# A mixture-of-experts encoder block: the router on raw rows, another order on three engines, and block 0's list ahead of the tables

## The chip, the cores and the metric

The kernel runs on one core of a Trainium2 chip. Its time is device time in microseconds (us) from the start to the end of the program on that core; a run is one execution, and the number given is the median of several. The engines are named as in the profile: PE (TensorE, matrix products), PEld (its weight loads), DVE (VectorE), ACT (ScalarE), POOL (GpSimd) and SP (SyncE, which here only issues DMAs).

## The reference

One layer works on 528 tokens (16 meta tokens and 512 others) of width 1024, in float32:

```
n    = rmsnorm(h, attn_norm); proj = n @ w_in           # 1024 x 3072
o    = stick_breaking_attention (8 heads) | differential_attention (4 heads)
h    = h + o @ w_out
xf   = rmsnorm(h, ffn_norm)
logits = xf @ w_router + b_router                       # 32 experts
top 4 of 32 per token, gates = softmax of the four logits
for each expert: act = clamped_swiglu(xf[tok] @ w1[e] + b1[e]); y = act @ w2[e] + b2[e]
h    = h + sum of gate * y over a token's four experts
out  = rmsnorm(h, final_norm), meta tokens dropped
```

w1 is 1024 x 2048 and w2 1024 x 1024 per expert, so the 32 experts' weights are 403 MB, and each is read once.

## The kernel before

The program is written by hand for each engine, in order; semaphores join them. It has four stages.

1. Projection and attention, from 0 to about 320 us. The change does not touch them beyond places of constants.
2. The tokens' stage, in four tiles of 128 tokens (t = 0 to 3). PE adds the differential heads' part of the output projection in eight units u of 512 columns (`out_tile`, L1447, two units a tile). DVE adds the residual (`token_rows`, L992), ACT squares and sums (L728) and takes the root by logarithm and exponential (`rsqrt`, L584 and L585), DVE refines the root in four small steps (L801 to L804) and writes the normed row, times the gain, to a stage buffer (L997). SP stores the raw rows to `accd` (L443) and the normed rows to `xfd` (L446), the table in memory that blocks gather from. PE turns the normed rows (`turn_tokens`, L1470), ACT copies them out of PSUM (L739), PE forms the 32 logits (`logits`, L1481), DVE adds the bias, finds the four largest and makes a 0/1 mask (L1008 to L1016), and from ACT's exponentials (L745) the gates in three bfloat16 parts with the token's number (L1018 to L1028).
3. The tables. PE counts tokens per expert and ranks each token within its expert (L1496 to L1500). DVE turns counts into numbers of 32-slot blocks; experts are put in an order ("places") through two small products (L1503, L1505); then tables by block are made (L1066 to L1082), after which `tab_ready` lets every engine read the number of blocks into a register.
4. The experts, 81 blocks of 32 slots. For block n: DVE compares ranks with slot numbers (`slot_list(n)`, L1097, L1101), PE's small product gathers token numbers and gates (`slot_product(n)`, L1527), DVE makes indices (`slot_rows(n)`, L1109 to L1122), POOL gathers rows from `xfd` (L535), PE turns them (`turn_x`, L1521), ACT copies (L751), PE multiplies by w1 (`up`, L1546) with a bias product at the end (L1553), DVE and ACT form the activation, PE turns it (L1583) and multiplies by w2 (`down`, L1573), DVE applies gates (L1142) and POOL adds rows to `accd` (L543). Lists run four blocks ahead; the list of a block and its product share one buffer, so `slot_list(n + 1)` waits for `slot_product(n)`.

Weights go through two buffers, one for even and one for odd places. SP issues an expert's four loads of w1 (L469) and two of w2 (L474) in the loop, each after PE has read that part for the buffer's last user. The first expert's weights and half of the second's w1 are loaded before the tables; the rest of the second's (L418 and L461) waits for `tab_ready` and block 0's gather.

## Time and profile before

| | |
|---|---|
| three runs | 1431.04 us median (1430.64 to 1434.6) |
| profiled execution | 1431.11 us, of which span 1429.3 |
| PE busy | 1302.9 us, 91% of the span |
| DVE, ACT, POOL busy | 670.1, 291.4, 284.3 us |
| mean granted clock of PE | 0.963 of full |
| DMA | 459.65 MB, mean 322 GB/s |

The span runs from the first to the last instruction. Busy shares are means over stages: a wait matters only where it ends last. A group's "idle before" is the time its engine stood still ahead of its instructions, with what ended most of it; "issue" there means that no wait of the profile explains it. SPq is the queue of DMA issues.

### The profile page before, as it was taken

To read this page: it belongs to the slowest core of one execution; us is meant where nothing else is said; L and a number is where in the kernel's file an instruction comes from. 1 tells how busy PE (TensorE), PEld (TensorE's weight loads), DVE (VectorE), ACT (ScalarE), POOL (GpSimd) and SP (SyncE) were. 2 spreads that over 40 slices of the span, in tenths; PEclk is the share of its full clock that TensorE was granted. 3 is DMA by queue.
4 is the path that set the end of the run, shared out by engine and by line. 5 is a ranking of instruction groups with operands and counts; after the bars stand their busy time and mean duration, and the time that the engine had idled before them with its cause. 6 is when DMAs were issued, how large, how long until landed. Compare 5 with 4: busy or idle time off the path is not lost.

```text
span 1429.3 us, 36690 instructions
## 1 busy us (share of the span) xinstructions
PE 1302.9 (91%) x13312; PEld 623.7 (44%) x13313; DVE 670.1 (47%) x2257; ACT 291.4 (20%) x578; POOL 284.3 (20%) x455
## 2 busy tenths in 40 slices
PE   4999999989288997899999999997999899999992
PEld 2655666555233442344444444442444344444441
DVE  3015333664644553355555555553455355555555
ACT  3102223432011111111111111111111111111113
POOL 5400000000012222122222222222222122222221
PEclk9999999999589999999999999998999999999996
DMA  9520001617478999999999998999999999999995
GB/s 317 157 50 1 1 1 63 236 27 312 158 313 337 415 417 418 419 416 416 417 418 417 417 417 319 378 413 417 419 416 417 422 416 417 417 418 417 415 416 185
DMA packets 59808, 459.65 MB, mean 322 GB/s; under 512 B 8420, under 2 KB 8804, under 8 KB 27012
## 3 DMA queue, kind: packets, MB, share of 16 engines
q1 hardware_dynamic: 51220, 436.63, 73.8%
q0 software_dynamic: 8176, 22.36, 6.0%
q8 instruction: 19, 0.31, 0.1%
q10 hardware_dynamic: 384, 0.26, 0.1%
q14 instruction: 9, 0.07, 0.0%
HBM read 440.72 MB, written 18.51 MB: 321 GB/s over the span
## 4 chain that ended last, share of the span: by engine, by line
PE 83%; DMA 9%; DVE 4%; issue 2%; ACT 1%; POOL 0%; SPq 0%; DVEq 0%; POOLq 0%; ACTq 0%
PE PS L1546 37%; PE PS L1573 19%; DMA sb_arena<-in_w 7%; PE PS L1227 4%; PE PS L1233 4%; PE PS L1583 2%; PE PS L1230 2%; PE PS L1231 2%; PE PS L1422 2%; PE PS L1447 1%; PE PS L1521 1%; PE PS L1589 1%; PE PS L1553 1%; PE PS L1329 1%; PE PS L1395 1%
## 5 line engine op out<-in xcount | busy, mean ns | idle before, releaser
L1546 PE MATMUL PS<-sb_arena,sb_work 128*32 128x512 f32 x5184 | 586.7, 603 | 35.3 <-DMA sb_arena<-in_w 28.6
L1546 PEld LDWEIGHTS PS<-sb_arena,sb_work 128*32 128x32 f32 x5184 | 174.2, 111 | 398.1 <-issue 347.4
L1573 PE MATMUL PS<-sb_arena,sb_work 128*32 128x256 f32 x5184 | 296.5, 380 | 4.6
L1129 DVE TENSOR_SCALAR sb_work<-PS 128x256 f32<-128x256 f32 x81 | 34.4, 425 | 395.8 <-PE PS L1553 395.8
L1573 PEld LDWEIGHTS PS<-sb_arena,sb_work 128*32 128x32 f32 x5184 | 166.3, 110 | 111.1 <-issue 19.4
L769 ACT ACTIVATE sb_work<-PS 128x256 f32<-128x256 f32 x81 | 31.1, 384 | 810.9 <-PE PS L1583 810.9
L1142 DVE TENSOR_SCALAR sb_work<-PS,sb_gates 32x256 f32<-32x256 f32 x324 | 155.2, 479 | 15.0 <-PE PS L1573 0.8
L534 POOL TENSOR_TENSOR sb_sm<-sb_sm 128x1 f32<-128x1 f32 x85 | 16.9, 199 | 676.9 <-DVE sb_gidx L1120 676.9
L1097 DVE TENSOR_SCALAR sb_slots<-sb_ca,sb_b,sb_rk 128x128 bf16<-128x128 f32 x344 | 96.5, 370 | 59.0 <-issue 58.2
L543 POOL DMA_INDIRECT accd<-sb_work,sb_sidc x81 | 111.1, 1371 | 12.5 <-issue 1.1
L767 ACT ACT_TABLE_LOAD x81 | 103.9, 1283 | 1.4
L535 POOL DMA_INDIRECT sb_work<-xfd,sb_gidx x85 | 86.2, 1014 | 14.0 <-issue 3.8
L1227 PE MATMUL PS<-sb_arena 128*128 128x512 f32 x128 | 60.1, 613 | 0.6 <-DVE sb_work L833 0.6
L1233 PE MATMUL PS<-sb_arena 128*128 128x512 f32 x128 | 58.6, 598 | 1.0 <-DVE sb_arena L851 1.0
L542 POOL TENSOR_TENSOR sb_sm<-sb_sm 128x1 f32<-128x1 f32 x81 | 15.7, 194 | 213.1 <-DVE sb_sidc L1144 213.1
L879 DVE TENSOR_TENSOR_SCAN sb_arena<-sb_arena 128x1344 f32<-128x1344 f32 x8 | 23.7, 2958 | 53.5 <-ACT sb_arena L639 53.5
L1583 PEld LDWEIGHTS PS<-sb_ca,sb_work 128*128 128x128 f32 x162 | 25.5, 206 | 53.2 <-issue 53.2
L1132 DVE TENSOR_TENSOR sb_work<-sb_work,PS 128x256 f32<-128x256 f32 x81 | 34.1, 421 | 29.7 <-ACT PS L756 29.6
L1583 PE MATMUL PS<-sb_ca,sb_work 128*128 128x128 f32 x162 | 40.9, 334 | 1.6 <-issue 1.5
L1230 PE MATMUL PS<-sb_arena 128*128 128x264 f32 x128 | 39.3, 389 | 0.0
L1231 PE MATMUL PS<-sb_arena 128*128 128x264 f32 x128 | 38.9, 386 | 0.0
L1521 PE MATMUL PS<-sb_ca,sb_work 128*128 128x128 f32 x166 | 33.9, 286 | 5.0 <-DMA sb_work<-xfd,sb_gidx 5.0
(246 smaller groups left out, 1165.8 us busy)
## 6 DMA issues: line engine op xcount, KB each, us to landing
sb_arena<-in_w SPq DMA_DIRECT2D x192, 2048.0 KB
sb_arena<-in_w_in SPq DMA_DIRECT2D x6, 2048.0 KB, 21.4
sb_arena<-in_x SPq DMA_DIRECT2D x8, 512.0 KB, 9.6
sb_arena<-in_w_out SPq DMA_DIRECT2D x2, 2048.0 KB, 13.1
accd<-sb_arena SPq DMA_DIRECT2D x4, 512.0 KB, 7.6
xfd<-sb_arena SPq DMA_DIRECT2D x4, 512.0 KB, 5.8
sb_arena<-accd SPq DMA_DIRECT2D x4, 512.0 KB, 5.0
out<-sb_arena SPq DMA_DIRECT2D x4, 512.0 KB, 3.5
```

What stands on the lines that cost most here:

```text
L535: pool.indirect_dma_start(out=xg[b], out_offset=None, in_=xfd, in_offset=bass.IndirectOffsetOnAxis(ap=gidx[:, b:b + 1], axis=0)).then_inc( ...
L543: pool.indirect_dma_start(out=acc, out_offset=bass.IndirectOffsetOnAxis(ap=sidc[0:SLOTS, b:b + 1], axis=0), in_=yb[b], in_offset=None, com ...
L767: act.preload_act_table(ACT.Sigmoid)
L1097: nc.vector.tensor_scalar(slots[:, t, :].rearrange("p (q s) -> p q s", s=SLOTS), ca[:, C_SLOT:C_SLOT + SLOTS].unsqueeze(1).to_broadcast([P ...
L1142: nc.vector.tensor_scalar(yb[b][:, c * QD:(c + 1) * QD], PS[rows, 4, 0:QD], gates[rows, bass.ds(n, 1)], None, ALU.mult).then_inc(y_ready, 1)
L1227: last = mm(PS[:, b, :], w[:, k, f * P:(f + 1) * P], nT[:, k, META:NKEY], **io)
L1230: mm(PS[:, b, 0:n], w[:, k, f * P:(f + 1) * P], nT[:, k, 0:n], **io)
L1231: last = mm(PS[:, b + 1, 0:n], w[:, k, f * P:(f + 1) * P], nT[:, k, n:NKEY], **io)
L1233: last = mm(PS[:, b, :], nT[:, k, META + f * P:META + (f + 1) * P], w[:, k, :], **io)
L1546: last = mm(PS[group(c), b, :].rearrange("p (a n) -> p a n", a=2), xT[:, k % 2, group(k // 2)], w[:, k, :, c, :], start=k == 0, stop=False)
L1573: last = mm(PS[group(n), 4, 0:QD], actT[:, k % 2, group(k // 2)], w[:, k, n * QD:(n + 1) * QD], start=False, stop=k == KT - 1)
L1583: last = nc.tensor.transpose(PS[:, 6, j * P:(j + 1) * P], pairs(gat[b], j), ident)
```

## The change

- *Raw rows.* The router's product works on `res`, the rows before the norm. The norm's gain vector is multiplied into the router's weights once (POOL, `wr` times `fcol`, a new small load), and the root's factor is applied to the logits as DVE reads them (first line of `choose`). Turning tokens no longer waits for the norm. The normed rows for `xfd` are now made by ACT (scale by the root) and POOL (times the gain).
- *Order.* Units of projection, turns and logits alternate on PE; DVE and ACT have their steps in a written-out order; `choose` and `weigh` are apart, with all 32 exponentials kept and masked. The last tile's turned rows are copied by DVE in two halves. The token numbers in `g6` are written by POOL at the start.
- *Tables.* Block 0 belongs to expert 0 from rank 0, so its list needs no table: DVE lists it (`slot_places(0, 0.0)`), PE multiplies, DVE makes its indices, and POOL gathers it while the tables are made. Slot numbers start from 1 so that a rank needs no subtraction. `slot_list(1)` comes before the last tables.
- *Start of the experts.* PE, ACT and POOL read the number of blocks later; on PE after block 0's `up`, and `slot_product(2)` is now behind it too. SP's wait for the gather is one for block 0's turn.
- Small buffers lie elsewhere in the work area.

```diff
-    a[:, C_SLOT:C_SLOT + SLOTS] = np.arange(SLOTS)
+    a[:, C_SLOT:C_SLOT + SLOTS] = 1 + np.arange(SLOTS)
...
-            sp.wait_ge(xg_in[0], 16)
+            sp.wait_ge(xT_done, 1)
...
+            pool.wait_ge(rout_in, 48)
+            nc.gpsimd.tensor_tensor(wr, wr, fcol.unsqueeze(2).to_broadcast([P, KT, NE]), ALU.mult)\
+                .then_inc(wr_ready, 1)
+            pool.wait_ge(gain_in, 32)
+            for t in range(TT):
+                pool.wait_ge(scaled, t + 1)
+                nc.gpsimd.tensor_tensor(stage[t % 2], stage[t % 2], gain, ALU.mult).then_inc(xf_ready, 1)
 
...
-            def token_norm(t):
+            def token_root(t):
                 act.wait_ge(h_ready, 2 * (t + 1))
                 if t >= 2:
-                    act.wait_ge(xfT_done, t - 1)
...
+            def token_scale(t):
+                act.wait_ge(root_ready, t + 1)
+                act.activation(stage[t % 2], res[:, t, :], ACT.Copy, scale=rinv[:, t:t + 1]).then_inc(scaled, 1)
+
+            def token_copy(t):
...
+            token_root(0)
+            token_scale(0)
+            token_root(1)
+            token_copy(0)
+            token_scale(1)
+            choice_exp(0)
+            token_root(2)
+            token_copy(1)
+            token_scale(2)
+            token_copy(2)
+            choice_exp(1)
+            choice_exp(2)
+            token_root(3)
+            token_scale(3)
+            choice_exp(3)
...
+            def choose(t):
                 dve.wait_ge(lg_done, t + 1)
                 if t == 0:
+                    dve.wait_ge(rout_in, 48)
+                row = lg[:, t, :]
+                nc.vector.scalar_tensor_tensor(row, PS[:, 6 + t % 2, 0:NE], rinv[:, t:t + 1], br,
+                                               ALU.mult, ALU.add).then_inc(lg_read, 1)
+                dve.wait_ge(lg_read, t + 1)
+                step(nc.vector.max(v8, row))
+                nc.vector.tensor_scalar(ntop[:, t:t + 1], v8[:, 0:1], -1.0, None, ALU.mult).then_inc(e4_in, 1)
+                step(nc.vector.max_index(i8u, v8, row))
                 step(nc.vector.tensor_copy(i8f, i8u[:, 0:TOPK]))
                 ie = ct[:, T_IE:T_IE + NE].unsqueeze(1).to_broadcast([P, TOPK, NE])
                 step(nc.vector.tensor_tensor(oh, i8f.unsqueeze(2).to_broadcast([P, TOPK, NE]), ie, ALU.is_equal))
+                step(nc.vector.tensor_reduce(gr[:, t, :], oh.rearrange("p k e -> p e k"), AX.X, ALU.add))
+                nc.vector.tensor_copy(msk[:, t, :], gr[:, t, :]).then_inc(msk_ready, 1)
+
+            def weigh(t):
+
+                row, part = e32[:, t, :], [g6[:, t, :, i] for i in range(3)]
                 dve.wait_ge(e4_ready, t + 1)
...
+            token_rows(0)
+            token_rows(1)
+            token_root(0)
+            token_rows(2)
+            token_rows(3)
+            token_root(1)
+            token_rows(4)
+            choose(0)
+            token_rows(5)
+            weigh(0)
+            token_root(2)
+            token_rows(6)
+            choose(1)
+            weigh(1)
+            choose(2)
+            token_rows(7)
+            for half in range(2):
+                dve.wait_ge(xfT_done, 2 * TT - 1 + half)
+                dve.wait_ge(lg_done, TT - 2)
+                nc.vector.tensor_copy(stT[1][:, 4 * half:4 * half + 4, :],
+                                      PS[:, 4 + half, :].rearrange("p (k n) -> p k n", k=4)).then_inc(xfT_ready, 1)
+            token_root(3)
+            choose(3)
+            weigh(2)
...
             step(nc.vector.tensor_copy(nb2[:, 0:1], nblk))
-            step(nc.vector.tensor_copy(nb2[:, 1:2], onesb[0:NE, 0:1]))
-            step(nc.vector.tensor_scalar(erep, onesb[0:NE, :], ca[0:NE, C_EXP:C_EXP + 1], None, ALU.mult))
-            step(nc.vector.tensor_copy(ee[:, 0:1], ca[0:NE, C_EXP:C_EXP + 1]))
+            weigh(3)
             dve.wait_ge(codes_done, 1)
...
+            dve.wait_ge(rank_done, 2)
+            step(nc.vector.scalar_tensor_tensor(rk[:, :, :], PS[:, 6, 64:64 + P].rearrange("p (t e) -> p t e", t=TT),
+                                                1.0, msk, ALU.add, ALU.mult))
+            dve.wait_ge(g6_ready, TT)
+            slot_places(0, 0.0)
+            step(nc.vector.tensor_scalar(at, ie0, place, None, ALU.is_equal))
+            dve.wait_ge(places_done, 1)
+            nc.vector.tensor_scalar(later, PS[0:NE, 7, 0:NE], place, None, ALU.is_ge).then_inc(nb_ready, 1)
+            step(nc.vector.memset(c6[:, :], 0.0))
+            slot_rows(0, 0, 0)
...
+            step(nc.vector.tensor_copy(egf[:, :], PS[:, 5, 256:256 + NG]))
+            step(nc.vector.tensor_copy(etab[:, :], egf[0:1, :]))
+            step(nc.vector.tensor_tensor(b64[:, :], ct[:, T_I32:T_I32 + NG], PS[:, 5, 128:128 + NG], ALU.subtract))
+            step(nc.vector.tensor_copy(prow, PS[0:1, 5, 0:NG]))
+            slot_list(1)
+            step(nc.vector.scalar_tensor_tensor(ptab[:, :], prow[:, 2:NG], float(AHEAD), prow[:, 0:NG - 2],
+                                                ALU.mult, ALU.add))
+            step(nc.vector.tensor_copy(order[:, :], PS[0:1, 4, NE:2 * NE]))
+            step(nc.vector.tensor_copy(btabi[:, :], PS[0:1, 4, 0:NE]))
+            nc.vector.memset(nx, 0.0).then_inc(tab_ready, 1)
+
...
+                for half in range(2):
+                    pe.wait_ge(h_ready, 2 * t + 1 + half)
+                    if t >= 1 and half == 0:
+                        pe.wait_ge(xfT_ready, t)
+                    for k in range(4 * half, 4 * half + 4):
+                        last = nc.tensor.transpose(PS[:, 4 + half, (k % 4) * P:(k % 4 + 1) * P],
+                                                   res[:, t, k * P:(k + 1) * P], ident)
+                    last.then_inc(xfT_done, 1)
...
+            for u in range(4):
+                out_part(u, 0, HF)
+            turn_tokens(0)
+            out_part(4, 0, HF)
+            logits(0)
+            out_part(5, 0, HF)
+            turn_tokens(1)
+            out_part(6, 0, HF)
+            turn_tokens(2)
+            logits(1)
+            out_part(7, 0, 2)
+            logits(2)
+            out_part(7, 2, HF)
+            turn_tokens(3)
+            logits(3)
...
+                if t == 0:
+                    pe.wait_ge(msk_ready, TT - 1)
                 for t2 in range(t):
                     mm(dst, onesb, msk[:, t2, :], start=t2 == 0, stop=False)
+                if t == TT - 1:
+                    pe.wait_ge(msk_ready, TT)
+                    for t2 in range(TT):
+                        last = mm(PS[0:NE, 7, 0:1], msk[:, t2, :], onesb[:, 0:1], start=t2 == 0, stop=t2 == TT - 1)
+                    last.then_inc(rank_done, 1)
...
+            slot_product(0)
             pe.wait_ge(nb_ready, 1)
             mm(PS[0:NE, 7, 0:2], later, nb2, start=True, stop=True).then_inc(bs_done, 1)
...
+            turn_x(0, 0, 0)
+            slot_product(1)
+            pe.wait_ge(xT_ready, 1)
+            up(0, 0, 0, 0)
             pe.wait_ge(tab_ready, 1)
             nb = pe.value_load(btabi[0:1, NE - 1:NE], min_val=1, max_val=MAXBLK)
-            slot_product(0)
-            turn_x(0, 0, 0)
-            slot_product(1)
-            pe.wait_ge(list_ready, 2)
             slot_product(2)
-            pe.wait_ge(xT_ready, 1)
-            up(0, 0, 0, 0)
             turn_x(1, 1, 0)
             slot_product(3)
```

How instructions stand on the engines, "[waits ...]" naming semaphores. First PE, end of the tokens' stage. L1447 is a unit of projection (four columns of k), L1481 logits, L1470 a turn. Before:

```order
L1447 MATMUL PS<-sb_arena 128x512 [waits h_ready]
L1447 MATMUL PS<-sb_arena 128x512 x3
L1481 MATMUL PS<-sb_arena 128x32 [waits e4_in,xfT_ready]
L1481 MATMUL PS<-sb_arena 128x32 x7
L1470 MATMUL PS<-sb_ca,sb_arena 128x128 [waits xfT_ready,xf_ready]
L1470 MATMUL PS<-sb_ca,sb_arena 128x128 x7
L1481 MATMUL PS<-sb_arena 128x32 [waits e4_in,xfT_ready]
L1481 MATMUL PS<-sb_arena 128x32 x7
L1470 MATMUL PS<-sb_ca,sb_arena 128x128 [waits xfT_ready,xf_ready]
L1470 MATMUL PS<-sb_ca,sb_arena 128x128 x7
L1481 MATMUL PS<-sb_arena 128x32 [waits e4_in,xfT_ready]
L1481 MATMUL PS<-sb_arena 128x32 x7
```

With the change (L1509 projection, L1548 logits, L1534 a turn, in halves):

```order
L1509 MATMUL PS<-sb_arena 128x512 [waits h_ready]
L1509 MATMUL PS<-sb_arena 128x512
L1548 MATMUL PS<-sb_arena 128x32 [waits xfT_ready,lg_read]
L1548 MATMUL PS<-sb_arena 128x32 x7
L1509 MATMUL PS<-sb_arena 128x512 x2
L1534 MATMUL PS<-sb_ca,sb_arena 128x128 [waits xfT_ready,h_ready]
L1534 MATMUL PS<-sb_ca,sb_arena 128x128 x3
L1534 MATMUL PS<-sb_ca,sb_arena 128x128 [waits h_ready]
L1534 MATMUL PS<-sb_ca,sb_arena 128x128 x3
L1548 MATMUL PS<-sb_arena 128x32 [waits xfT_ready,lg_read]
L1548 MATMUL PS<-sb_arena 128x32 x3
L1548 MATMUL PS<-sb_arena 128x32 [waits xfT_ready]
```

The last turn and last logits had nothing between them and waited on the norm (`xf_ready`); now half units of projection stand between the logits of tiles 1 and 2 and the last turn, which waits for the raw rows (`h_ready`), and the last logits come in two halves.

Second DVE, from the experts' places on. Before (L1060 the key of places, L1063 to L1071 ends of experts, from L1073 tables):

```order
L1060 TENSOR_SCALAR sb_work<-sb_ca,sb_work 32x32 [waits dve_step]
L1061 TENSOR_SCALAR sb_work<-sb_work 32x32
L1063 TENSOR_SCALAR sb_work<-PS,sb_work 32x32 [waits places_done,dve_step]
L1066 COPY sb_work<-PS 32x1 [waits bs_done]
L1067 CAST sb_work<-sb_work 32x1 [waits dve_step]
L1068 TENSOR_TENSOR sb_work<-sb_work 32x1 [waits dve_step]
L1069 TENSOR_SCALAR sb_work<-sb_work 32x102 [waits dve_step]
L1070 TENSOR_SCALAR sb_work<-sb_work 32x102 [waits dve_step]
L1071 TENSOR_TENSOR sb_work<-sb_work 32x102 [waits dve_step]
L1073 COPY sb_egf<-PS 128x102 [waits tab_done]
L1074 COPY sb_work<-PS 1x102 [waits dve_step]
L1075 SCALAR_TENSOR_TENSOR sb_ptab<-sb_work 1x100 [waits dve_step]
```

With the change (L1115 the key, L1157 ranks, L1121 and L1125 the list, L1161 and L1163 ends, L1140 on the indices):

```order
L1115 TENSOR_SCALAR sb_work<-sb_ca,sb_work 32x32 [waits dve_step]
L1157 SCALAR_TENSOR_TENSOR sb_rk<-PS,sb_work 128x128 [waits rank_done]
L1121 TENSOR_SCALAR sb_slots<-sb_ca,sb_rk 128x128 [waits g6_ready,dve_step]
L1121 TENSOR_SCALAR sb_slots<-sb_ca,sb_rk 128x128 x3
L1125 COPY sb_g6c<-sb_g 128x24
L1161 TENSOR_SCALAR sb_work<-sb_work 32x32
L1163 TENSOR_SCALAR sb_work<-PS,sb_work 32x32 [waits places_done,dve_step]
L1164 MEMSET sb_c 128x9
L1140 COPY sb_c<-PS 128x6 [waits list_done,dve_step]
L1142 TENSOR_SCALAR sb_c<-sb_c 128x1 [waits list_step]
L1144 TENSOR_SCALAR sb_c<-sb_c,sb_ca 128x1
```

Block 0's list and indices have moved from behind all tables to a place ahead of them.

Third PE, around blocks 0 and 1. L1527 is a list's product, L1546 and L1553 block 0's first expert product, L1521 the turn of block 1's rows, L1532 a register load. Before:

```order
L1527 MATMUL PS<-sb_g6c,sb_slots 128x6 [waits slots_ready,list_ready]
L1527 MATMUL PS<-sb_g6c,sb_slots 128x6 x3
L1546 MATMUL PS<-sb_arena,sb_work 32x512 [waits w1_full00,xT_ready]
L1546 MATMUL PS<-sb_arena,sb_work 32x512 x7
...
L1553 MATMUL PS<-sb_ball,sb_selb 32x512 [waits sel_ready]
L1553 MATMUL PS<-sb_ball,sb_selb 32x512 x3
L1521 MATMUL PS<-sb_ca,sb_work 128x128 [waits xT_ready,xg_in1]
L1521 MATMUL PS<-sb_ca,sb_work 128x128
L1527 MATMUL PS<-sb_g6c,sb_slots 128x6 [waits slots_ready]
L1527 MATMUL PS<-sb_g6c,sb_slots 128x6 x3
L1532 TENSOR_LOAD sb_ptab
```

With the change (L1588, L1626 and L1633, L1607, L1612; L1679 is the load of the number of blocks):

```order
L1626 MATMUL PS<-sb_arena,sb_work 32x512 [waits w1_full00,xT_ready]
L1626 MATMUL PS<-sb_arena,sb_work 32x512 x7
...
L1633 MATMUL PS<-sb_ball,sb_selb 32x512 [waits sel_ready]
L1633 MATMUL PS<-sb_ball,sb_selb 32x512 x3
L1679 TENSOR_LOAD sb_btabi [waits tab_ready]
L1679 ISA x2
L1588 MATMUL PS<-sb_g6c,sb_slots 128x6 [waits slots_ready]
L1588 MATMUL PS<-sb_g6c,sb_slots 128x6 x3
L1607 MATMUL PS<-sb_ca,sb_work 128x128 [waits xT_ready,xg_in1]
L1607 MATMUL PS<-sb_ca,sb_work 128x128
L1588 MATMUL PS<-sb_g6c,sb_slots 128x6 [waits slots_ready]
L1588 MATMUL PS<-sb_g6c,sb_slots 128x6 x3
```

Behind block 0 there are now a register load and two list products instead of one, list 2's and list 3's, with block 1's turn between.

## Rows read from the trace of the kernel before

**Rows 1.** The page: clock and DMA by 36 us slices, costliest group.
```profile
PEclk9999999999589999999999999998999999999996
DMA  9520001617478999999999998999999999999995
...
L1546 PE MATMUL PS<-sb_arena,sb_work 128*32 128x512 f32 x5184 | 586.7, 603 | 35.3 <-DMA sb_arena<-in_w 28.6
```

**Rows 2.** Busy times by 30 us windows; columns as in the first row.
```profile
core 0: us, PE busy (x) PEld busy (x) DVE busy (x) ACT busy (x) POOL busy (x), PEclk, DMA share, GB/s
440.00:470.00 30.00, 29.89 (x348) 11.84 (x338) 12.27 (x44) 4.49 (x8) 6.01 (x10) 0.97 0.81 326
...
860.00:890.00 30.00, 29.83 (x368) 13.09 (x364) 14.01 (x51) 6.21 (x12) 7.47 (x12) 1.00 0.77 296
```

**Rows 3.** The same view in windows of 4 us.
```profile
372.00:376.00 4.00, 0.58 (x14) 0.46 (x14) 3.42 (x17) 0.00 (x0) 0.00 (x0) 0.50 1.01 426
380.00:384.00 4.00, 0.57 (x5) 0.30 (x5) 2.87 (x14) 0.00 (x0) 0.00 (x0) 0.50 0.00 2
...
444.00:448.00 4.00, 3.94 (x48) 1.65 (x44) 0.93 (x3) 0.86 (x3) 0.00 (x0) 1.00 0.24 102
```

**Rows 4.** Timeline of the DMA-issuing queue (start us, us, queue, line).
```profile
392.41 0.82 SPq L418 DMA_DIRECT2D sb_arena<-in_w  x2
...
453.83 1.49 SPq L469 DMA_DIRECT2D sb_arena<-in_w  x2
```

**Rows 5.** Timeline of PE, blocks 3 and 4; in brackets the idle time before.
```profile
437.25 9.20 PE L1546 MATMUL PS<-sb_arena,sb_work 128*32 128x512 f32 x64 [5.48 <-issue]
...
451.17 7.05 PE L1546 MATMUL PS<-sb_arena,sb_work 128*32 128x512 f32 x64
```

**Rows 6.** Chain of waits, the tokens' stage (start us, us, what).
```profile
320.16 14.00 PE PS L1447 x32
334.16 0.87 PE PS L1470 x8
335.04 6.87 PE PS L1447 x16
341.90 1.72 PE PS L1481 x16
```

**Rows 7.** Timeline of DVE: the choice of the last 128 tokens.
```profile
369.94 0.19 DVE L1008 TENSOR_TENSOR sb_arena<-PS,sb_arena 128x32 f32<-128x32 f32 x1 [2.46 <-PE PS L1481]
...
371.69 0.18 DVE L1016 CAST sb_work<-sb_arena 128x32 bf16<-128x32 f32 x1
```

**Rows 8.** Timeline of ACT: turned copy, squares, last step of the root.
```profile
345.09 1.00 ACT L739 ACTIVATE sb_arena<-PS 128x1024 f32<-128x1024 f32 x1
349.51 1.06 ACT L728 ACTIVATE sb_arena<-sb_arena 128x1024 f32<-128x1024 f32 x1 [3.42 <-DVE sb_arena L992]
...
351.01 0.20 ACT L585 ACTIVATE sb_sm<-sb_sm 128x1 f32<-128x1 f32 x1
```

**Rows 9.** DMA view, 331 to 333 us; the last number is us to landing.
```profile
xfd<-sb_arena SPq DMA_DIRECT2D x1, 512.0 KB, 14.2
```

**Rows 10.** Timeline of DVE: a register load, and block 0's indices.
```profile
384.95 0.07 DVE L1147 MEMSET sb_c<- 128x9 f32 x1 [0.88 <-issue]
...
388.38 0.21 DVE L1120 TENSOR_SCALAR sb_gidx<-sb_c 128x1 int32<-128x1 f32 x1
```

**Rows 11.** Chain of waits from block 0's gather to block 1.
```profile
389.49 2.84 DMA sb_work<-xfd,sb_gidx
...
396.65 8.98 PE PS L1546 x64
...
407.56 2.76 PE PS L1546 x21
```

**Rows 12.** DMA view, 399 to 402 us, the gather queue.
```profile
q0 software_dynamic: 48, 0.13, 10.9%
```

**Rows 13.** Groups by line, POOL: its widest two-input operation.
```profile
L511 POOL TENSOR_TENSOR sb_arena<-sb_arena,sb_ball 32x1024 f32<-32x1024 f32 x3 | 7.2, 2404 | 0.3
```

255 lines of the change are left out of this document (108 added, 147 removed).

## Prediction, written before the changed kernel ran

> **What bounds the kernel now.** I read the page first, then windows, then the chain. The page's slices show a long stretch, from about 460 us to the end, in which the DMA engines are full and PE is nearly so; its costliest group, the first expert product, lost 35.3 us idle, 28.6 of them to weights [rows 1]. So two things bound the experts' stage, PE and the weight stream, and the question is where each last waited for the other. The 30 us windows answer it: from 860 to 890 us PE is full while the DMA share is 0.77 (the stream waits for PE to free a buffer), and from 440 to 470 it is 0.81 [rows 2]. The fine windows find the earliest such gap, DMA share 0.24 at 444 to 448 us [rows 3], and the queue's timeline ends it: the loads for the fourth expert are issued at 453.83, once PE has read the buffer in block 4 [rows 4], whose product begins at 451.17 [rows 5]. From there on both engines run on each other. Before there, nothing is full: the stream stood idle, so it is PE's blocks 0 to 4 that set when everything later happens. **A microsecond won before block 4 is won at the end**, and the sum only has to say how much earlier block 4 starts.
>
> Block 0 starts at 396.65 [rows 11] and waits for a chain with no slack: PE projects and turns tokens (320.16 to 343.6, [rows 6]), then DVE and PE hand one another short work. In 372 to 376 us DVE is busy 3.42 us with 17 instructions, in 380 to 384 us 2.87 us with 14 [rows 3]: 31 in 8 us, 0.26 us per link, and PE idles at clock 0.5, the lower of its two levels, 1.2 GHz. This latency chain is what the change rewrites.
>
> **Term 1, the tokens' stage.** Before, the last choice starts at 369.94 and its mask is cast at 371.69 to 371.87, 1.93 us after it began [rows 7]. After, I walk PE's new list. Four units of projection take 14.00, a full turn 0.87, one unit half of 6.87, so 3.44, logits of 128 tokens 1.72 [rows 6]. 320.16 + 14.00 + 0.87 + 3.44 (unit 4) + 1.72 (logits 0) + 3.44 (unit 5) + 0.87 (turn 1) + 3.44 (unit 6) = 347.9. All that these wait for is earlier: the raw rows are turned, so no turn waits for the norm, and the copy of turn 0 is ready at about 337.8. Then one wait is left. ACT's third square writes over the stage of tile 0 and must wait for that tile's store, which landed 14.2 us after its issue at 332 [rows 9], behind 8 MB of weights; the store is now issued some 2 us later (POOL multiplies by the gain) but queues behind the same weights, so I keep 346.2. Square and root take 1.7 (349.51 to 351.21), the copy behind them 1.0 [rows 8]: 349.0, a stall of 1.1 on PE. Turn 2, logits 1, half of unit 7, logits 2, other half: 0.87 + 1.72 + 1.72 + 1.72 + 1.72 from 349.1 gives 356.9. DVE's add (0.7), squares and root on ACT (1.7) and DVE's refining (four links, 0.9) come to 360.3; on the other branch half a turn and two copies of 0.7 each feed the last half of the logits, done at about the same time. Choice 1.93: the last mask is there at 362.5. Gain 371.87 - 362.5 = 9.4. PE is denser until 357, so its clock can hardly fall earlier than it did.
>
> **Term 2, from the last mask to block 0's indices.** Before: 371.87 to 388.59 = 16.7 [rows 7, 10], with all tables, two register loads and the list in it. After, DVE's row holds 39 instructions: 7 weigh(2), 3 counts, 2 code and key, 2 bf16 copies, 7 weigh(3), 3 rank, place and key, 1 rank table, 5 slots, 3 small ones, 6 of the list. At 0.24 to 0.26 us each plus about 0.3 for PE's product this is 9.7. The two weigh calls sit ahead of waits that PE has already met, so they cost about 3 us on the path, yet less than the tables did. Gain 7.0. Indices at 372.2, gather issued 0.9 later (388.59 to 389.49), 373.1. The four tables' stores are no limit: POOL's two-input operation of 1024 columns takes 2.4 us [rows 13], so the last store goes out near 365 and lands by 371. If its price grew with partitions (32 there, 128 here) it would be 9.6 us, four in a row from 332 end at 370.4, the store lands near 375.5, and the end comes 2.4 us later.
>
> **Term 3, the gather.** Before it flew alone, 2.84 us [rows 11]. After, it meets the 4 MB of w2 loads that are issued right behind the last store and run until about 377. The next gather did meet such a stream: issued at 395.21, its packets ran only between 399 and 402 [rows 12], 6.5 us. Bounds 2.84 and 6.5; I take 5.4, since the stream ends meanwhile. Loss 2.6: it lands at 378.5. The Trainium skill, "DMA: Bandwidth & Descriptors", queues and rings, says that each DMA engine takes turns between queues packet by packet. By that rule a gather of few packets should be held up by one or two weight packets only, about 1 us, and land near 377, which would make the end 1.5 us earlier; the gather of [rows 12] disagrees.
>
> **Term 4, landing to block 0.** Before 392.33 to 396.65 = 4.3, because the product of list 2 was ahead of block 0. After only the turn (0.7), ACT's copy and their hops, 1.4; list 1, ahead of it on PE, is ready at about 377.5. Gain 2.9. Block 0 starts at 379.9, 16.7 us earlier (9.4 + 7.0 - 2.6 + 2.9). It ends 9.2 later, at 389.2, since its clock starts low as before.
>
> **Term 5, a new serial wait between block 0 and block 1.** PE's row now has, behind block 0: register load, product of list 2, turn 1, product of list 3, register load and branch. List 3 is written by DVE only after it has read the product of list 2, and before the change block 0's 9 us hid that. Now nothing does: register load 0.9 (DVE's took 0.88, [rows 10]), product 0.3, DVE's rows 1.3, list 3 1.8 (1.12 of slots, 0.48 of register load and the copy), product 0.3, load and branch 1.2: 5.8. Before, block 0's end at 405.9 to block 1 at 407.56 [rows 11] was 1.7. Loss 4.1. Block 1 at 395.0, 12.6 earlier. Queued behind PE here is everything; DVE's first activation only waits with it.
>
> **Term 6, the clock.** PE is idle for more than 5 us there. In block 3 it was idle 5.48 and the product took 9.20; the next took 7.05 at full clock [rows 5]. Block 1 took 7.07 before, so I charge 2.15; bounds 0 and 2.15. Block 1 ends 10.4 us earlier.
>
> Block 2 follows without a gap, and block 3's idle 5.48 stays. The stream's second expert is issued after the tables and block 0's turn, about 379.5 in place of 392.41 [rows 4], 20 us of loads, so it is done near 400 and block 3, near 427, does not wait. POOL's token columns, the extra router load and the longer constants lie beside waits: POOL's own first work after the attention stage is block 0's gather, and the loads go out with the first experts'. I take 0, bounds 0 and 0.5.
>
> **Sum.** The profiled execution took 1431.11 (span 1429.3 plus 1.8 around it; the runs' median is 1431.04, the same). 1431.1 - 9.4 - 7.0 + 2.6 - 2.9 + 4.1 + 2.15 = **1420.6 us**.
>
> **Rivals.** *A, more is won:* the gather flies as if alone (2.6 back), PE's clock stays (2.15 back), DVE's links go at 0.24 (0.8 back): 1415.0. For it: loads may drain first. Against: [rows 12], [rows 5].
>
> *B, the stream decides:* if the weights bound everything from their second start, only 392.41 - 379.5 = 12.9 counts, 1418.2. Against it: DMA share 0.24 and 0.00 in [rows 3].
>
> *C, one more stall for instructions:* PE's idle 5.48 ahead of block 3 is put down to nothing it waits for, and block 3 is the first to run the other parity's copy of the code, behind a taken branch, with the DMA engines full [rows 5]. After the change PE reaches the code of block 0 and 1 with the stream running, while before it sat idle with quiet DMA engines first. One such stall costs 5.48 + 2.15 = 7.6: 1428.2. The Trainium skill ("Runtime: NRT & Kernel Launch", instruction fetch mechanics) says that prefetch is sequential and that a taken branch outside of the fetched pages waits for a DMA. By that rule block 3's stall stays and the straight code of block 0 is safe; the trace agrees as far as block 3 goes.
>
> *D, slower:* the same stall in two places, ahead of block 0's product and at block 1's branch, 15.2: 1435.8. It decides once stalls sum to more than 10.5 us. Nothing in the trace shows two.
>
> **Chances.** Forecast 0.65 (its own range 1416 to 1425), A 0.15, B 0.05, C 0.11, D 0.04. A measurement of this kernel tells apart about 0.3%, 4.3 us: faster (forecast, A, B) 0.85, same (C) 0.11, slower (D) 0.04. Range 1413 to 1428.5: A with room below for both weigh calls being cheaper, C at the top.
>
> **What would show it.** The last mask near 362.5; block 0's indices near 372 and its product near 380; PE idle about 5 us between blocks 0 and 1 with DVE's list 3 as releaser, and block 1's product at 9.2; the same gap in the DMA windows ahead of block 4's release, now near 443; all later waits of PE for weights as long as before. The forecast is wrong if the block 0 start moves by under 12 us, or if the later idle time of the expert products grows.

## The result, and the profile after

| | before | after |
|---|---|---|
| median | 1431.39 us (1429.61 to 1434.6, 8 runs) | 1420.83 us (1418.35 to 1426.62, 8 runs) |
| profiled execution | 1431.11 us, span 1429.3 | 1421.65 us, span 1419.7 |
| mean granted clock of PE | 0.963 | 0.972 |

The ratio is 0.9928, 95% interval 0.9912 to 0.9944: faster by 0.7%. The forecast was 1420.6. In a second set, beside some of its variants, the same kernel had 1421.46 us (1419.45 to 1423.19, 5 runs), ratio 0.9939 (0.9926 to 0.9951).

The page of the kernel after, clock and DMA by slices and the costliest group, against [rows 1]:

```profile
PEclk9999999999699998999999999999999999999997
DMA  8520000607678999999999998999999999999995
...
L1626 PE MATMUL PS<-sb_arena,sb_work 128*32 128x512 f32 x5184 | 587.2, 604 | 36.9 <-DMA sb_arena<-in_w 29.9
```

The first expert product lost 36.9 us idle where it had lost 35.3, its waits for weights 29.9 where they had been 28.6. The prediction had named growing idle time there as a sign against it. It cost nothing: from block 4's start to the end of the span it is 978.3 us after and 978.1 before, so what was won ahead of block 4 was still there at the end. Windows of the kernel after (PE, PEld, DVE, ACT and POOL busy, PEclk, DMA share, GB/s), against [rows 3]:

```profile
436.00:440.00 4.00, 3.94 (x64) 2.28 (x60) 2.59 (x11) 2.25 (x4) 0.00 (x0) 1.00 0.02 8
```

Ahead of the release of the next weight buffer the DMA share was 0.02: the stream waited for PE, as at 444 to 448 us in [rows 3]. The queue of DMA issues, against [rows 4]:

```profile
382.06 0.81 SPq L423 DMA_DIRECT2D sb_arena<-in_w  x2
...
443.77 5.22 SPq L475 DMA_DIRECT2D sb_arena<-in_w  x4
```

The second expert's loads are issued 10.35 us earlier, the release in block 4 10.06 us earlier. PE's timeline after, against [rows 5, 11] (L1576 counts tokens, L1607 turns a block's rows, L1588 is a list's product, L1626 a block's first expert product):

```profile
365.55 0.27 PE L1576 MATMUL PS<-sb_work 128*32 128x1 bf16 x4 [3.55 <-DVE sb_work L1052]
...
381.27 0.70 PE L1607 MATMUL PS<-sb_ca,sb_work 128*128 128x128 f32 x2 [5.23 <-DMA sb_work<-xfd,sb_gidx]
...
382.44 9.36 PE L1626 MATMUL PS<-sb_arena,sb_work 128*32 128x512 f32 x64 [0.39 <-ACT sb_work L784]
...
391.95 0.25 PE L1588 MATMUL PS<-sb_g6c,sb_slots 128*128 128x6 bf16 x4
...
395.43 0.25 PE L1588 MATMUL PS<-sb_g6c,sb_slots 128*128 128x6 bf16 x4 [2.88 <-DVE sb_g6c L1125]
396.87 8.77 PE L1626 MATMUL PS<-sb_arena,sb_work 128*32 128x512 f32 x64 [1.19 <-ACT sb_work L784]
...
410.36 7.05 PE L1626 MATMUL PS<-sb_arena,sb_work 128*32 128x512 f32 x64
...
427.83 8.86 PE L1626 MATMUL PS<-sb_arena,sb_work 128*32 128x512 f32 x64 [5.51 <-issue]
...
441.41 7.05 PE L1626 MATMUL PS<-sb_arena,sb_work 128*32 128x512 f32 x64
```

Block 0 is 14.2 us earlier than in [rows 11] (396.65), block 1 10.7 (407.56), and blocks 3 and 4 9.4 and 9.8 against [rows 5]. Three more views show what stood behind it. The chain of waits after, the store of the first tile and block 0's gather, against [rows 9, 11]:

```profile
335.11 12.08 DMA xfd<-sb_arena
...
374.99 6.23 DMA sb_work<-xfd,sb_gidx
```

ACT after, its third square, waiting for that store, against [rows 8]:

```profile
347.27 1.06 ACT L744 ACTIVATE sb_arena<-sb_arena 128x1024 f32<-128x1024 f32 x1 [5.27 <-DMA xfd<-sb_arena]
```

DVE after, the last choice (L1042 to L1052) and block 0's indices, and POOL's multiply beside it, against [rows 7, 10, 13]:

```profile
358.32 0.18 DVE L1052 CAST sb_work<-sb_arena 128x32 bf16<-128x32 f32 x1
...
361.89 0.25 DVE L1042 SCALAR_TENSOR_TENSOR sb_arena<-PS,sb_sm,sb_arena 128x32 f32<-128x32 f32 x1 [0.17 <-PE PS L1548]
...
363.30 0.38 DVE L1051 TENSOR_REDUCE sb_arena<-sb_arena 128x32 f32<-128x128 f32 x1
363.70 1.79 DVE L1052 CAST sb_work<-sb_arena 128x32 bf16<-128x32 f32 x1
...
373.88 0.21 DVE L1151 TENSOR_SCALAR sb_gidx<-sb_c 128x1 int32<-128x1 f32 x1
```
```profile
362.98 2.48 POOL L544 TENSOR_TENSOR sb_arena<-sb_arena 128x1024 f32<-128x1024 f32 x1 [9.45 <-ACT sb_arena L751]
```

The mask's cast takes 1.79 us in the last tile and 0.18 in the third. It ends at 365.49, POOL's multiply at 365.46.

### The profile page after: what moved, and what is told of

The parts are those of the page before. It is cut to its first block, busy times and chain, and to the rows that moved or that the text cites. A ratio compares the mean times of both kernels' runs of the same rounds, so it can differ in the third digit from the quotient of the medians.

```text
span 1419.7 us, 36680 instructions
## 1 busy us (share of the span) xinstructions
PE 1299.2 (92%) x13312; PEld 620.4 (44%) x13313; DVE 660.7 (47%) x2241; ACT 294.6 (21%) x577; POOL 296.1 (21%) x464
## 4 chain that ended last, share of the span: by engine, by line
PE 82%; DMA 10%; DVE 4%; issue 2%; ACT 1%; POOL 0%; SPq 0%; DVEq 0%; POOLq 0%; ACTq 0%
PE PS L1626 37%; PE PS L1653 19%; DMA sb_arena<-in_w 7%; PE PS L1290 4%; PE PS L1296 4%; PE PS L1663 2%; PE PS L1293 2%; PE PS L1294 2%; PE PS L1485 2%; PE PS L1607 1%; PE PS L1669 1%; PE PS L1633 1%; PE PS L1392 1%; PE PS L1458 1%; DMA xfd<-sb_arena 1%
## 5 line engine op out<-in xcount | busy, mean ns | idle before, releaser
L1626 PE MATMUL PS<-sb_arena,sb_work 128*32 128x512 f32 x5184 | 587.2, 604 | 36.9 <-DMA sb_arena<-in_w 29.9
L1626 PEld LDWEIGHTS PS<-sb_arena,sb_work 128*32 128x32 f32 x5184 | 174.7, 111 | 399.8 <-issue 348.8
L1196 DVE TENSOR_SCALAR sb_work<-PS 128x256 f32<-128x256 f32 x81 | 34.3, 424 | 398.8 <-PE PS L1633 398.8
L551 POOL TENSOR_TENSOR sb_sm<-sb_sm 128x1 f32<-128x1 f32 x85 | 16.7, 197 | 552.5 <-DVE sb_gidx L1151 552.5
L1121 DVE TENSOR_SCALAR sb_slots<-sb_ca,sb_b,sb_rk 128x128 bf16<-128x128 f32 x340 | 96.1, 367 | 59.2 <-issue 59.2
L552 POOL DMA_INDIRECT sb_work<-xfd,sb_gidx x85 | 85.8, 1009 | 14.1 <-issue 3.8
L1607 PE MATMUL PS<-sb_ca,sb_work 128*128 128x128 f32 x166 | 33.9, 286 | 5.2 <-DMA sb_work<-xfd,sb_gidx 5.2
```

The costliest lines, as they stand in the source:

```text
L552: pool.indirect_dma_start(out=xg[b], out_offset=None, in_=xfd, in_offset=bass.IndirectOffsetOnAxis(ap=gidx[:, b:b + 1], axis=0)).then_inc( ...
L1121: nc.vector.tensor_scalar(slots[:, t, :].rearrange("p (q s) -> p q s", s=SLOTS), ca[:, C_SLOT:C_SLOT + SLOTS].unsqueeze(1).to_broadcast([P ...
L1626: last = mm(PS[group(c), b, :].rearrange("p (a n) -> p a n", a=2), xT[:, k % 2, group(k // 2)], w[:, k, :, c, :], start=k == 0, stop=False)
```

## Experiments

Each kernel is the changed one with the edit shown. "Set" means kernels that ran together and share their runs of the kernel before. Only one set holds the changed kernel too (the second one above, with the mask's product, w2 behind the gather and the squares apart), so across sets the ratios are to be compared.

One thing bears on all of them: PE's projection of the tokens' stage began anywhere from 318.22 to 322.10 us in the profiles of the changed kernel and its variants, a spread that the edits do not explain. Where it matters, the start is given.

### Raw rows undone, order kept

```diff
-            nc.gpsimd.tensor_tensor(wr, wr, fcol..., ALU.mult)
+            nc.gpsimd.tensor_copy(wr, wr)
...
-    scalar_tensor_tensor(row, PS[...], rinv[:, t:t + 1], br, ...)
+    scalar_tensor_tensor(row, PS[...], 1.0, br, ...)
...
             token_rows(7)
+            token_root(3)
             for half in range(2):
...
-            token_root(3)
             choose(3)
...
-                    pe.wait_ge(h_ready, 2 * t + 1 + half)
+                    pe.wait_ge(xf_ready, t + 1)
...
-                        res[:, t, k * P:(k + 1) * P], ident)
+                        stage[t % 2][:, k * P:(k + 1) * P], ident)
```

DVE's order is not quite kept: the last tile's root now stands ahead of the two copies of its turned rows, which wait for the norm here.

> The changed kernel with one part undone: PE turns the normed rows (it waits for POOL's last step of the norm), the router's weights are not multiplied by the gain, and the logits are not scaled. The order on every engine stays. The output is unchanged. Own theory (turning raw rows is what takes the norm off the path): PE stalls at turn 2 for about 3.5 us more and the last turn waits for root (2.0), scale (1.1) and POOL's 2.4 us, about 6 us more; the 1.6 us that DVE's last mask lost beside POOL may come back. Together about +8 us: last mask near 373, PE's block 0 product near 390, time about 1428.8. Rival (the new order alone gives the gain, the norm is hidden by it): 0 to +2 us, 1421 to 1423.

Measured: 1434.88 us (1431.41 to 1438.56, 12 runs), ratio to before 1.0027 (1.0016 to 1.0039). That is 14 us above the changed kernel, not 8. PE and clock in this kernel:

```profile
352.70 1.97 PE L1534 MATMUL PS<-sb_ca,sb_arena 128*128 128x128 f32 x8 [4.21 <-POOL sb_arena L544]
...
364.56 3.76 PE L1509 MATMUL PS<-sb_arena 128*128 128x512 f32 x4
...
375.33 1.97 PE L1534 MATMUL PS<-sb_ca,sb_arena 128*128 128x128 f32 x8 [7.00 <-POOL sb_arena L544]
...
397.13 8.72 PE L1626 MATMUL PS<-sb_arena,sb_work 128*32 128x512 f32 x64
```
```profile
352.00:356.00 4.00, 3.30 (x16) 3.30 (x17) 0.00 (x0) 1.02 (x1) 0.65 (x1) 0.59 0.32 131
356.00:360.00 4.00, 4.00 (x13) 2.89 (x13) 1.83 (x11) 0.32 (x1) 0.00 (x0) 0.50 0.00 0
```

Both stalls are there as expected (4.21 and 7.00 us). What I left out is that the first of them lets the clock fall to 0.50, so half a unit of projection takes 3.76 us in place of 1.96, and every step up to the last logits takes about twice as long. The last mask is there at 382.94, not near 373: 17.5 us later than in the changed kernel and 11.1 later than before the change. Block 0's list ahead of the tables and the shorter way from the landing to block 0 win 10.6 of these 11.1 back, so block 0 is 0.5 later than before the change (14.7 later than in the changed kernel), and the new wait behind it makes block 1 3.4 later. So the new order loses in the tokens' stage unless the rows are raw, and without them the whole change gains nothing. The rival is out.

### Tables first again, block 0's list behind them, twice

```diff
-            dve.wait_ge(rank_done, 2)
-            step(nc.vector.scalar_tensor_tensor(rk[:, :, :], ...
-            slot_places(0, 0.0)
...
-            slot_rows(0, 0, 0)
...
-            slot_list(1)
...
             nc.vector.memset(nx, 0.0).then_inc(tab_ready, 1)
+            dve.wait_ge(rank_done, 2)
+            step(nc.vector.scalar_tensor_tensor(rk[:, :, :], ...
+            slot_places(0, 0.0)
...
+            slot_rows(0, 0, 0)
+            slot_list(1)
...
-            slot_product(0)
             pe.wait_ge(nb_ready, 1)
...
+            slot_product(0)
             turn_x(0, 0, 0)
```

> The changed kernel with another part undone: block 0's rank table, list, product and indices stand behind all tables, list 1 behind them. Own theory: the indices are some 4.3 us later (near 378.4 in place of 374.1), but by then the loads of w2 have drained (their packets ended near 379), so the gather flies near its lone 2.84 us and lands near 382.1 in place of 381.2: +0.9 us, time about 1421.7. Rival (the gather takes 6.2 us wherever it is, so the lateness passes through whole): +4.3 us, 1425.1.

Measured: 1425.91 us (1421.02 to 1427.65, 7 runs), ratio 0.9963 (0.9951 to 0.9976): by the median the rival's value. But the profiled run has what the own theory says. Its chain:

```profile
378.17 0.23 DVE sb_gidx L1151
...
379.29 2.85 DMA sb_work<-xfd,sb_gidx
382.18 0.72 PE PS L1606 x2
```

The gather flew 2.85 us, block 0 began at 383.36, 0.92 later than in the changed kernel, and block 4 at 441.20, 0.2 earlier. Its tokens' stage was 0.6 earlier than in the changed kernel (third turn at 349.45 for 350.04), so at block 0 the other order costs 1.5 us, not 0.9. So it ran again:

> The kernel with all tables ahead of block 0's list once more. The first time its profiled run had the lone gather (2.8 us) and block 4's first product at 441.2, as the changed kernel, but its median was 4.5 to 5 us above the changed kernel's. Theory 1 (the order costs only 0.9 us, the rest was the draw of runs and of PE's granted clock): median near 1422 this time, mean clock 0.970. Theory 2 (this order makes PE's clock rise later or fall more often in most runs, which one profile did not show): median near 1425 again, mean clock near 0.968, and perhaps a profile with block 4 later than 442.

Measured: 1422.81 us (1421.31 to 1426.05, 6 runs), ratio 0.9934 (0.9918 to 0.9950), mean clock 0.971; the gather 2.81 us again, block 0 again 1.5 us later counted from the third turn, block 4 at 441.60. The profiled run is the slowest of the six (1426.05 us), and it lost its time behind block 4: from there to the end it took 982.4 us, in the first profile of the same kernel 977.8. The first theory fits, but the two intervals do not overlap, so the size of it stays open between 0 and some 4 us; that the lone gather takes 2.8 us is shown twice.

### The stream's second start later

```diff
             sp.wait_ge(xT_done, 1)
+            sp.wait_ge(up_done, 1)
             w1_load(1, 1)
```

> The changed kernel with SP's loads for the second expert held until block 0's first product is done, about 10 us later (near 392 in place of 382); nothing else moves. Own theory (up to block 4 the stream has slack, only PE's blocks count): no change, 1420.8 within 0.5; the DMA gap ahead of block 4's release shrinks by these 10 us or vanishes. Rival (from its second start the stream decides): +9.9 us, 1430.7.

Measured: 1424.09 us (1421.72 to 1425.95, 6 runs), ratio 0.9952 (0.9938 to 0.9966). The loads went out at 392.16, the DMA share at 436 to 440 us was still 0.13, block 4 began at 440.47, 0.94 earlier than in the changed kernel, and the first later product that waits for weights at 553.74 (changed kernel 554.36). The stream had its slack and +9.9 is out. The expectation of no change within 0.5 us was missed all the same: the span is 2.8 us longer, and from block 4 to the end it is 982.0 us in place of 978.3. Behind the waits for weights near 1115 us two parts of a product ran at half clock in this kernel, in the changed one only the first. The second part, in this kernel and in the changed one:

```profile
1122.49 3.64 PE L1627 MATMUL PS<-sb_arena,sb_work 128*32 128x512 f32 x16 [1.52 <-DMA sb_arena<-in_w]
```
```profile
1123.04 1.92 PE L1626 MATMUL PS<-sb_arena,sb_work 128*32 128x512 f32 x16 [1.73 <-DMA sb_arena<-in_w]
```

The last 40 us had another such dip. A late stream is not needed for it: the tables first, run again, took 982.4 us from block 4 on and list 2 inside 981.5, with the stream's start where it was, while the other profiles have 977.8 to 979.5. Whether a later stream makes such dips more frequent is open.

### List 2's product inside block 0's first product, at two places

```diff
                     if k % 2 == 1:
                         last.then_inc(w1_read, 1)
+                    if k == 5 and isinstance(g, int) and g == 0:
+                        slot_product(2)
...
             nb = pe.value_load(btabi[0:1, NE - 1:NE], min_val=1, max_val=MAXBLK)
-            slot_product(2)
             turn_x(1, 1, 0)
```

> The changed kernel with the product of list 2 inside block 0's first product (behind its sixth column group of eight, so that DVE makes list 3 while PE multiplies). Own theory (the serial chain product 2, DVE's rows, list 3, product 3 is what stands between blocks 0 and 1): the gap of 4.85 us goes to about 1.7 and block 1 runs at full clock (8.77 to 7.07 us): -4.9 us, time about 1416. Rival (the register load and the taken branch hold PE there, not the list): no change.

Measured: 1421.3 us (1419.36 to 1422.54, 5 runs), ratio 0.9931 (0.9918 to 0.9944). In the time, nothing. The trace:

```profile
390.20 0.25 PE L1588 MATMUL PS<-sb_g6c,sb_slots 128*128 128x6 bf16 x4
...
393.68 0.25 PE L1588 MATMUL PS<-sb_g6c,sb_slots 128*128 128x6 bf16 x4 [0.72 <-DVE sb_g6c L1125]
...
395.12 7.08 PE L1626 MATMUL PS<-sb_arena,sb_work 128*32 128x512 f32 x64 [1.18 <-ACT sb_work L784]
```

From list 2's product to list 3's it is 3.48 us, as in the changed kernel (391.95 to 395.43). The chain moved as a whole, by the 1.75 us that its start moved, and block 1's product ran at full clock. Block 4 began at 438.71, 2.7 us earlier; from there to the end it took 981.5 us in place of 978.3, dips behind later weight waits, which gave it back in this execution.

The gap's last wait is not list 3's product but ACT's copy. DVE and ACT in the changed kernel:

```profile
394.07 1.28 DVE L1121 TENSOR_SCALAR sb_slots<-sb_ca,sb_b,sb_rk 128x128 bf16<-128x128 f32 x4 [0.48 <-issue]
...
395.28 0.35 DVE L1196 TENSOR_SCALAR sb_work<-PS 128x256 f32<-128x256 f32 x1
```
```profile
395.67 0.39 ACT L789 ACTIVATE PS<-sb_work 128x256 f32<-128x256 f32 x1 [11.61 <-DVE sb_work L1196]
395.99 0.37 ACT L784 ACTIVATE sb_work<-PS 128x256 f32<-128x256 f32 x1
```

DVE makes list 3 (L1121) ahead of the first step of block 0's activation (L1196); ACT's sigmoid (L789) waits for that step, and ACT's copy of block 1's turned rows (L784), for which block 1's product waits, stands behind the sigmoid. So the chain from list 2's product to DVE's list 3 is what fills the gap, and it holds block 1 through the orders of DVE and ACT. The place was too late to hide it. The copy ahead of the sigmoid was not tried. Hence the same edit with `k == 3`:

> As the kernel with list 2's product inside block 0's first product, but two groups of columns earlier (behind the fourth of eight), since from that product to list 3's product it took 3.48 us in both and the sixth group was only 1.75 us ahead of the end. Own theory (that chain of 3.48 us is the whole gap): it is now hidden, block 1 starts 1.7 us behind block 0's end as before the change (2.6 with the later place, 4.85 without), 3.1 us earlier than in the changed kernel, and its product runs at full clock, 7.07 us in place of 8.77: 4.8 us in all at block 1's end, time about 1416.5 (less of it where other dips of the clock differ). Rival (something else, ACT's copy or the branch, is next at 2.6 us): as the later place, 1418 to 1421.

Measured: 1420.35 us, ratio 0.9914 (0.9889 to 0.9939), six runs in two groups: 1416.1, 1416.31, 1417.61 and 1423.09, 1423.5, 1425.69. The profiled run is of the upper one. From the last bias product to block 1 it is 1.7 us, and block 1's product takes 7.07, as expected; the 1.7 us are the activation's first step, the sigmoid and the copy, as before the change. What makes it long lies earlier:

```profile
348.82 1.06 PE L1534 MATMUL PS<-sb_ca,sb_arena 128*128 128x128 f32 x8 [1.31 <-ACT sb_arena L757]
...
351.86 3.76 PE L1509 MATMUL PS<-sb_arena 128*128 128x512 f32 x4
```
```profile
352.00:356.00 4.00, 4.00 (x9) 1.93 (x8) 3.20 (x17) 0.32 (x1) 0.33 (x1) 0.50 0.32 131
356.00:360.00 4.00, 4.00 (x16) 3.48 (x16) 0.91 (x6) 0.32 (x1) 0.00 (x0) 0.50 0.00 0
```

Behind PE's stall of 1.31 us ahead of its third turn the clock was at 0.50 from 352 on, with PE busy all the time; in the changed kernel's profile nearly the same stall (1.27) was followed by full clock. That turn was 1.2 us earlier than in the changed kernel's profile, and block 0's indices 4.9 us later: 6.1 us for one dip, of which 5.2 are left at block 0's start, since the gather took 5.33 us in place of 6.23. The lower group fits the expected 1416.5, but no profile of one of its runs was taken, so it is not shown that its runs lack the dip.

### The mask by a two-input product, and by the reduction itself

```diff
-   nc.vector.tensor_copy(msk[:, t, :], gr[:, t, :])
+   nc.vector.tensor_tensor(msk[:, t, :], gr[:, t, :], gr[:, t, :], ALU.mult)
```

> The changed kernel with the mask written by a product of two inputs (the 0/1 row with itself) in place of a one-input copy. Own theory: the copy of the last mask took 1.79 us in place of 0.18 because DVE's one-input copy within the work area was held until POOL's multiply ended, while two-input steps beside POOL were not held; so the mask is there 1.6 us earlier, block 0's indices too (372.5 in place of 374.1), and the time is 1.6 us lower, about 1419.2. Rival 1 (DVE is held by POOL whatever it does there, or the wait is POOL's semaphore traffic): the mask as late as now, no change. Rival 2 (the gather ends with the stream of w2, near 379 to 381, whenever it is issued): indices 1.6 us earlier, block 0 not, no change.

Measured: 1421.02 us (1419.63 to 1424.75, 6 runs), ratio 0.9937 (0.9924 to 0.9949), the same as the changed kernel in its set (0.9939). The product was held as well:

```profile
362.85 1.81 DVE L1052 TENSOR_TENSOR sb_work<-sb_arena 128x32 bf16<-128x32 f32 x1
```

My theory, that only the one-input copy is held, is wrong. Next, no conversion at all:

```diff
-   step(tensor_reduce(gr[:, t, :], oh..., ALU.add))
-   nc.vector.tensor_copy(msk[:, t, :], gr[:, t, :]).then_inc(msk_ready, 1)
+   tensor_reduce(msk[:, t, :], oh..., ALU.add).then_inc(msk_ready, 1)
...
+   dve.wait_ge(msk_ready, t + 1)
-   scalar_tensor_tensor(row, row, 1.0, gr[:, t, :], ...)
+   scalar_tensor_tensor(row, row, 1.0, msk[:, t, :], ...)
```

> The changed kernel with the mask written by the reduction itself, so that the conversion that was held until POOL's multiply ended is gone, and the gates' first step reads that mask. Theory 1 (only the conversion to bf16 from work rows is held by POOL; the reduction, which ran beside POOL in 0.37 us, is not): the last mask is there 1.8 us earlier, near 363.7 in place of 365.5, block 0's indices near 372.2, the time 1.8 us lower, about 1419.2. Theory 2 (the next step in line, the gates' product, is then the one that is held until POOL ends): PE gets the mask earlier, but DVE's row starts no earlier, no change. Theory 3 (the gather's end does not move with its issue): indices earlier, block 0 not.

Measured: 1422.34 us (1420.97 to 1425.08, 6 runs), ratio 0.9934 (0.9918 to 0.9950): no change.

```profile
363.62 0.38 DVE L1052 TENSOR_REDUCE sb_work<-sb_arena 128x32 bf16<-128x128 f32 x1
363.91 1.92 DVE L1060 SCALAR_TENSOR_TENSOR sb_arena<-sb_arena,sb_work 128x32 f32<-128x32 f32 x1
```

The mask was there near 364.0, but the next step, the gates' product, was held until POOL's multiply ended at 365.79, and the indices came at 374.34. Theory 2 is right. In the traces three forms are held beside POOL's multiply: a plain copy, and two products with both inputs in SBUF. Two are not: the reduction, and, beside POOL's earlier multiplies, the choice's first step, whose main input is in PSUM (0.25 us in all tiles). The Trainium skill, "SBUF — State Buffer", section "Who interferes with whom", says that a DVE instruction with two SBUF inputs contends with a GpSimd instruction that reads SBUF, and one in a mode that uses both port pairs with any, and that the one issued later waits for the whole of the other. The rows of the products, the reduction and the first step agree with it; the copy's does if it ran in such a mode, which no row here shows. I did not weigh it in the prediction, though the change put POOL's multiply beside the last choice.

### The first expert's w2 behind block 0's gather

```diff
-            for c in range(2):
-                sp.dma_start(w2d(0, c), w2v(0, c)).then_inc(w2_full[0][c], 16)
             sp.wait_ge(h_out, 16 * (TT + 1))
             for t in range(TT):
                 sp.wait_ge(xf_out[t], 32 if t == TT - 1 else 16)
+            sp.wait_ge(xg_in[0], 16)
+            for c in range(2):
+                sp.dma_start(w2d(0, c), w2v(0, c)).then_inc(w2_full[0][c], 16)
             sp.wait_ge(tab_ready, 1)
```

> The changed kernel with the first expert's loads of w2 issued once block 0's gather has landed, not ahead of it. Own theory (the gather took 6.2 us in place of 2.84 because it shares the DMA engines with these loads): the gather lands near 377.9, block 0's product then waits for list 1's product on PE and starts near 379.9 in place of 382.4, 2.5 us earlier, and the loads are still done before block 0's second product needs them: about 1418.3. Rival (the gather's time has another cause, or the stream, now later by 8 MB and 10 us, gives the gain back): no change in the time.

Measured: 1418.59 us (1415.6 to 1420.14, 5 runs), ratio 0.9910 (0.9897 to 0.9923), 2.9 us below the changed kernel of its set.

```profile
378.49 0.70 PE L1608 MATMUL PS<-sb_ca,sb_work 128*128 128x128 f32 x2 [1.83 <-DMA sb_work<-xfd,sb_gidx]
380.12 0.27 PE L1589 MATMUL PS<-sb_g6c,sb_slots 128*128 128x6 bf16 x4 [0.93 <-DVE sb_g6c L1126]
```

The gather was issued at 375.62 and had landed by 378.49; block 0 then waited for list 1's product and began at 380.32. As expected, 2.1 us earlier, though its indices were 0.6 later. The interval lies below that of the changed kernel in the same set (0.9926 to 0.9951), so this gain is clear of the noise.

These loads explain more than term 3. SP issued them in the changed kernel behind the last tile's store:

```profile
367.13 1.01 SPq L458 DMA_DIRECT2D sb_arena<-in_w  x2
```

The gather landed 14.1 us later, and in the other seven profiles in which they go ahead of it 13.8 to 14.4 us after their issue. That holds for list 2 in the middle too, where the gather was issued 0.9 us later behind them than elsewhere (8.8 for 7.8 to 7.9) and took 5.33 us. In the changed kernel 46 of the gather's 48 packets ran between 378 and 380 us, while the DMA share fell from 1.01 (378 to 379) to 0.40. So by these rows block 0 waits for the end of w2's loads, not for its indices, and these loads go out 2.4 us later than before the change (364.74), behind POOL's multiply and its store. It follows that earlier indices alone, as the mask's two edits aimed at, could have won nothing; only one profile varies the distance, so this is argued more than shown.

### ACT's squares apart

```diff
+        squares = arena[:, o + HF * T:o + HF * T + D]
...
-                if t >= 2:
-                    act.wait_ge(xf_out[t - 2], 16)
-                act.activation(stage[t % 2], res[:, t, :], ACT.Square, accum_out=ss[:, t:t + 1])\
+                act.activation(squares, res[:, t, :], ACT.Square, accum_out=ss[:, t:t + 1])\
...
             def token_scale(t):
                 act.wait_ge(root_ready, t + 1)
+                if t >= 2:
+                    act.wait_ge(xf_out[t - 2], 16)
```

> The changed kernel with ACT's squares written to a place of their own, so that ACT's third square no longer waits for the store of tile 0 (it waited 5.27 us; the store landed 12.08 us after its issue). Own theory: PE's stall of 1.27 us ahead of its third turn goes, the last mask and all behind it come 1.3 us earlier (up to 2 with the copy held by POOL at another place): about 1419.5. Rival (the next wait in line, ACT's scale into the same stage, takes its place): no change.

Measured: 1419.74 us (1415.72 to 1420.76, 5 runs), ratio 0.9917 (0.9904 to 0.9931), 1.7 us below the changed kernel, though the two intervals overlap. PE's third turn no longer stalls:

```profile
347.05 1.04 PE L1535 MATMUL PS<-sb_ca,sb_arena 128*128 128x128 f32 x8
```

Block 0 began at 379.63, 2.8 us earlier. Of that 1.5 us were there ahead of the edit's place (POOL's first multiply began at 331.19, not 332.74), so 1.3 is the edit's in this trace, as expected.

### The changed kernel again

> The changed kernel once more, unchanged, beside the others on one chip. If the excess of the kernel with the late stream (3 us where none was expected) and of the one with the tables first (5 us where 0.9 was) comes from the chip or the day, this one is near 1424 too. If it is from those kernels, this one is at 1420.8 within 1 us. Block 4's first product starts at 441.4 within 0.5 in its trace by either.

Measured: 1421.46 us (above), so neither chip nor day. In its trace the projection began 1.3 us earlier (319.61), but a dip of the clock behind the third turn's stall of 0.97 us took 1.6 back:

```profile
351.20 3.48 PE L1509 MATMUL PS<-sb_arena 128*128 128x512 f32 x4
```

The half unit took 3.48 us in place of 1.96; block 0 began at 382.67, 0.2 later. Its block 4 began at 439.59, 1.8 us earlier than in the first profile: block 0's product took 8.19 us in place of 9.36, blocks 1's and 3's 8.41 and 8.56. The bound of 0.5 us was wrong; from block 0 on the clock moved block 4 by some 2 us, and this is the noise against which the smaller edits stand.

### Four edits together

> Four edits together: list 2's product in the middle of block 0's, w2's loads behind block 0's gather, ACT's squares apart, the mask written by the reduction. If each keeps its worth (4.8, 2.9, 1.7 and 1.8 us) and nothing new ends last, block 0's product starts near 376.5 and the time is about 1410. Rival (the second expert's loads and the first expert's w2 now crowd into the same stretch, or list 1's product holds block 0): half of it, about 1415.

Measured: 1413.52 us (1412.12 to 1415.12, 4 runs), ratio 0.9873 (0.9853 to 0.9894). In its set the kernel before had 1433.13, so by the ratios it is 0.5 to 0.7% below the changed kernel, between what was expected (1410) and the rival (1415). PE's timeline and the window ahead of block 4:

```profile
373.38 0.70 PE L1611 MATMUL PS<-sb_ca,sb_work 128*128 128x128 f32 x2 [1.80 <-DMA sb_work<-xfd,sb_gidx]
375.04 0.27 PE L1592 MATMUL PS<-sb_g6c,sb_slots 128*128 128x6 bf16 x4 [0.96 <-DVE sb_g6c L1129]
...
386.99 1.50 PE L1630 MATMUL PS<-sb_arena,sb_work 128*32 128x512 f32 x12 [1.19 <-ACT sb_work L786]
```
```profile
428.00:432.00 4.00, 4.00 (x68) 2.15 (x64) 3.15 (x14) 1.06 (x1) 1.44 (x3) 1.00 0.40 109
```

Block 0 began at 375.24, 7.2 us earlier than in the changed kernel, block 1 9.9, block 4 (430.83) 10.6, the span is 9.4 shorter. Of the 7.2, 2.7 are not the edits': the projection began at 318.22 for 320.93. This is the fastest version run. Block 0 now waits for list 1. The DMA gap ahead of block 4's release is down to a part of 4 us (0.40), and from block 4 to the end it is 979.5 us, 1.2 more than in the changed kernel, so little more can probably be won in this way before the stream is the bound.

## Why the prediction was right

The working held in kind: what is won ahead of block 4 passes through to the end (978.1 us from there before, 978.3 after). By its steps, gains in us up to block 2's start:

| step | predicted | measured |
|---|---|---|
| 1, last mask | 9.4 (at 362.5) | 6.4 (at 365.49) |
| 2, mask to block 0's indices | 7.0 | 8.1 (8.60 for 16.7) |
| 3, the gather | -2.6 | -3.4 (6.23 for 2.84) |
| 4, landing to block 0 | 2.9 | 3.1 (1.22 for 4.3) |
| 5, between blocks 0 and 1 | -4.1 | -3.5 |
| 6, block 1's clock | -2.15 | -1.25 |
| sum | 10.4 | 9.4 |

That the median, 1420.83, lies 0.2 from the forecast is in part luck: terms 1 and 3 came 3.8 us short, the others 2.8 us better than charged, and the kernel's own runs lie 8 us apart.

*Term 1* was mis-sized by 3.0. The tokens' stage began 0.77 later in this execution (320.93 for 320.16); 1.6 is the mask's cast behind POOL, which the walk along PE's list did not have; 0.3 is DVE's last add, which began behind the third tile's choice (358.41, PE's part done at 358.11). The stall of 1.1 at the third turn was 1.27. The sum's own steps end at 362.2 (360.3 plus 1.93), not 362.5. "Its clock can hardly fall earlier than it did" is false as a rule: it holds in the profile after and fails in three others: list 2 in the middle (6.1 us), the changed kernel again and the late stream (1.6 us each). *Term 2* was 1.1 too small; the bound that it carried, a multiply of 9.6 us, did not come (2.35 to 2.48). *Term 3* was 0.8 too small, and its cause is shown: two kernels in which the gather does not meet w2's loads (tables first, w2 behind) have it at 2.8 to 2.9 us. It was summed as if it were independent of term 2, and by the rows above it is not: the landing follows the end of w2's loads, so that what the indices gain the gather would lose. The Trainium skill's rule that was weighed there ("DMA: Bandwidth & Descriptors", section "Queues, rings and completion order": queues served in turn, packet by packet) gave the prediction an estimate of about 1 us of delay; these rows disagree. *Term 5*: the chain up to list 3 was as described, and moving its start moved it whole. Its end was not: the prediction put 1.2 us to a register load and a branch of PE and said that "DVE's first activation only waits with it". In the trace that activation step stands behind list 3 and is on the path, with ACT's sigmoid and copy behind it (1.19 us of idle time on PE, put down to that copy). It charged 5.8 us to the gap and it was 4.85, since PE's register load ahead of list 2's product cost nothing: list 2's product began at 391.95, as the last bias product ended. The rest of the 3.5 is block 0's product, 0.4 slower. *Term 6*: block 1's product was 1.7 slower; 0.4 of it came back, since behind it PE had idled 0.38 us before the change and no longer did.

The clock is thus real but not additive. The kernels with list 2 inside had block 1's product at 7.07, but idled 0.8 to 1.5 us more behind it.

*Rivals.* A's 1415.0 needed the lone gather and the full clock; neither came by itself; with edits for both, and two more, the time was 1413.52. B is excluded by the late stream. C and D: no new stall for instructions; idle time put down to nothing stood only ahead of block 3 (5.51, before 5.48), at its old place. The branch into block 1 cost nothing that the trace shows.

What the prediction lacked is the spread: the changed kernel's runs lie 8 us apart. The profiles show three sources. The stage's start varies by 4 us. The clock dips behind the third turn's stall in three of the ten profiles that have a stall of 0.7 to 1.3 us there, and costs 1.6, 1.6 and 6.1 us; the size of the stall does not decide it (1.11, 0.97 and 1.31 with a dip, up to 1.27 without). And from block 4 on three profiles need 981.5 to 982.4 us, the others 977.8 to 979.5. The two kernels without the stall show no such dip, one profile each; whether it is this that sets their runs closer together is not shown.

## What to carry to other kernels

Where neither PE nor the stream is full yet, walk the chain from engine to engine and pass its gain through to the end; then look for what the new order sets beside what. Here three neighbours counted: weight loads beside a gather that everything waits for (2.1 us at block 0), a scratch write tied to a store (1.3 us in the trace), and POOL's multiply beside DVE's products, which held DVE for 1.6 us, though no edit of it changed the time. Before working on one chain, look for what really ends last: the gather landed with the end of the weight loads, and not at a fixed time behind its indices. A stall of a microsecond in a stretch where PE is otherwise full can cost several through the clock, and in only some runs, so judge such an edit by its trace and by many runs, not by one of them.

## What was not expected of the hardware

- A 128x32 step of DVE took 1.79 to 1.92 us in place of 0.18 beside POOL's two-input multiply of 128x1024 (2.48 us), ending within 0.06 us of it.
- A gather of one block took 6.23 us with 4 MB of weight loads ahead of it (5.33 to 6.57 in eight profiles), and 2.81 to 2.85 alone. Issued 4.3 us later, when these loads had ended, it landed 0.9 us later.
- PE's granted clock fell from 1.00 to 0.50 behind a stall of 1.31 us in one execution and behind one of 0.97 us in another, and not behind one of 1.27 us in a third.
